# The decay's low-rank input on four column groups, summed by the next product

## The reference

```python
h = x * (1.0 + scale[:, None, :]) + shift[:, None, :]
(a_q, a_k, a_v, a_g, g_q, g_k, g_v, g_af, g_ab, ...) = jnp.split(h @ p['w_in'], pts, axis=-1)

def log_decay(pa, a2, ab):            # pa: tokens x 16, a2: 16 x 256
    z = (pa @ a2 + ab).astype(jnp.float32)
    return heads(jax.nn.log_sigmoid(z) / GLA_GATE_TEMP, GLA_DK)

... log_decay(paf, a2_f, ab_f), log_decay(pab, a2_b, ab_b)
```

## Time and profile before

| | |
|---|---|
| median of 3 runs | 1673.78 us (1673.46 to 1674.21) |
| the profiled execution's own time | 1673.7 us |
| its span | 1671.9 us |
| TensorE busy | 1612.8 us, 96% of the span |
| VectorE, ScalarE, GpSimd busy | 616.8, 423.3, 193.2 us |
| mean granted TensorE clock | 0.982 of full |
| bytes moved | 183.71 MB |

### The profile page before, as it was taken

The page is one execution under the profiler, slowest core; times in us unless marked ns, Lnnn a source line. Parts: engine busy times, 40 slices in busy tenths (PEclk is TensorE's granted clock), DMA queues, the critical chain, the costliest instruction groups (busy, mean ns, idle before and its releaser), DMA issues.

```text
span 1671.9 us, 17017 instructions
## 1 busy us (share of the span) xinstructions
PE 1612.8 (96%) x6880; PEld 1056.8 (63%) x6880; DVE 616.8 (37%) x1398; ACT 423.3 (25%) x808; POOL 193.2 (12%) x272
## 2 busy tenths in 40 slices
PE   5999999999999999999999999889999999999997
PEld 2544454455444444464776888478899847889883
DVE  1033342464200002522334311355577215567821
ACT  3114325432200000003243320034232213423320
POOL 0132100120010011121201102110100011010001
PEclk7999999999999999999999999989999999999999
DMA  9324332211112113321232343513322223432230
GB/s 389 149 101 157 123 123 94 84 52 40 60 76 76 75 51 142 130 101 54 101 116 86 115 170 119 195 51 137 116 101 76 104 102 135 151 107 95 76 126 38
DMA packets 16930, 183.71 MB, mean 110 GB/s; under 512 B 2258, under 2 KB 2514, under 8 KB 4564
## 3 DMA queue, kind: packets, MB, share of 16 engines
q1 hardware_dynamic: 16852, 182.62, 29.0%
HBM read 181.56 MB, written 1.05 MB: 109 GB/s over the span
## 4 chain that ended last, share of the span: by engine, by line
PE 93%; ACT 3%; DMA 2%; DVE 1%; POOL 0%; issue 0%; POOLq 0%; SPq 0%; ACTq 0%; DVEq 0%
PE ps L665 90%; PE ps L712 4%; DMA arena<-in_wf 2%; ACT arena L1136 1%; DVE arena L1515 0%; ACT L1469 0%; ACT L1467 0%; DVE arena L1512 0%; POOL arena L2054 0%; POOL arena L2058 0%; ACT arena L1467 0%; ACT arena L1368 0%; ACT L1370 0%; ACT L1368 0%; ACT arena L1352 0%
## 5 line engine op out<-in xcount | busy, mean ns | idle before, releaser
L665 PE MATMUL ps<-arena 128*128 128x256 f32 (+7 forms) x6396 | 1561.7, 426 | 26.9 <-DMA arena<-in_wf 17.2
L665 PEld LDWEIGHTS ps<-arena 128*128 128x128 f32 (+3 forms) x6396 | 1001.6, 186 | 551.7 <-issue 435.8
L2054 POOL TENSOR_TENSOR arena<-arena 128x256 f32<-128x256 f32 (+4 forms) x214 | 162.7, 779 | 1049.7 <-DVE arena L1515 648.8
L1515 DVE SCALAR_TENSOR_TENSOR arena<-arena 128x256 f32<-128x256 f32 (+3 forms) x443 | 211.1, 535 | 154.2 <-ACT arena L1241 41.1
L1136 ACT ACTIVATE arena<-ps 128x512 f32<-128x512 f32 (+2 forms) x274 | 142.6, 537 | 421.2 <-PE ps L665 398.2
L1515 DVE SCALAR_TENSOR_TENSOR arena<-arena,ps 128x256 f32<-128x256 f32 (+2 forms) x136 | 64.3, 482 | 389.6 <-PE ps L665 291.0
L1509 DVE TENSOR_TENSOR arena<-arena 128x512 f32<-128x512 f32 (+14 forms) x156 | 89.0, 592 | 120.5 <-ACT arena L1136 35.2
L712 PE MATMUL ps<-arena 128*128 128x128 f32 x480 | 75.7, 289 | 22.8 <-ACT arena L1136 18.2
L712 PEld LDWEIGHTS ps<-arena 128*128 128x128 f32 x480 | 58.4, 147 | 52.3 <-issue 27.1
L1307 ACT ACTIVATE arena<-ps 128x512 f32<-128x512 f32 (+1 forms) x24 | 13.5, 562 | 248.5 <-PE ps L665 248.5
L1512 DVE TENSOR_SCALAR arena<-arena 128x256 f32<-128x256 f32 (+9 forms) x181 | 64.9, 393 | 24.2 <-POOL arena L2054 17.0
(11 more groups left out here) (87 smaller groups left out, 306.0 us busy)
## 6 DMA issues: line engine op xcount, KB each, us to landing
arena<-in_wf SPq DMA_DIRECT2D x70, 2048.0 KB, 8.0
arena<-in_wf SPq DMA_DIRECT2D x20, 1024.0 KB, 6.7
arena<-in_wf SPq DMA_DIRECT2D x2, 1152.0 KB, 11.2
arena<-in_xinT SPq DMA_DIRECT2D x1, 2048.0 KB, 22.2
arena<-in_xin SPq DMA_DIRECT2D x4, 512.0 KB, 5.6
arena<-in_rp SPq DMA_DIRECT2D x2, 1024.0 KB, 10.3
arena<-in_consts SPq DMA_DIRECT2D x1, 1476.0 KB, 14.8
out<-arena SPq DMA_DIRECT2D x2, 512.0 KB, 2.6
```

The lines of the kernel that those rows point to most:

```text
L665: return e.matmul(o, l, r, start=start, stop=stop, skip_group_check=True)
L1515: return e.scalar_tensor_tensor(out=o, in0=x, scalar=s, in1=y, op0=op0, op1=op1)
L2054: return e.tensor_tensor(o, x, y, op)
```

## The change

The 8 products of `lr` are no longer added up in one place: product k goes to PSUM partitions 32 (k mod 4) to 32 (k mod 4) + 31, so each of the four column groups of the array has two of them, and the bank holds four partial sums below each other. ScalarE copies all 128 partitions to `TH2`. `z` multiplies all 128 partitions; its stationary tile holds the decay matrices four times below each other, so the product also adds the four parts. That tile stands in 512 new columns of the parameters, `PZ`, zero where nothing is named; `PM` keeps what the gating unit needs. The parameter transfer of each layer grows from 128x552 to 128x1064 values, and what stands behind `par` in SBUF moves by 512 columns.

```diff
-PA_BADA, PA_AB, PA_ON, PA_LG, PA_PM, PA_SW, PA_W = 0, 24, 28, 29, 40, 552, 1064
+PA_BADA, PA_AB, PA_ON, PA_LG, PA_PM, PA_PZ, PA_SW, PA_W = 0, 24, 28, 29, 40, 552, 1064, 1576
...
         PM = par[:, PA_PM:PA_PM + 512]
+        PZ = par[:, PA_PZ:PA_PZ + 512]
...
                         elif n == "lr":
-                            ins = feat(b, weights(f"a{l}kv", 8), 256, hT, 0, 512, [hk(l, k) for k in range(8)], 32)
+
+                            w = weights(f"a{l}kv", 8)
+                            for k in range(8):
+                                p.wait_ge(*hk(l, k))
+                                r = 32 * (k % 4)
+                                ins = mm(b[r:r + 32, :], w[:, k, 256:288], hT[:, k, :], k < 4, k >= 4)
...
-                        mm(bank("gla", l, "z", 2 * hp + d), PM[0:32, 256 * d + 128 * hp:256 * d + 128 * hp + 128],
-                           TH2[0:32, :], True, True).then_inc(gl_z.hit(l, 2 * hp + d), 1)
+                        mm(bank("gla", l, "z", 2 * hp + d), PZ[:, 256 * d + 128 * hp:256 * d + 128 * hp + 128],
+                           TH2, True, True).then_inc(gl_z.hit(l, 2 * hp + d), 1)
...
                         elif n == "lr":
-                            ins = copy(TH2[0:32, :], b[0:32, :])
+                            ins = copy(TH2, b)
...
-        pa[l][0:16, PA_PM:PA_PM + 256] = I["gla_a2_f"][l]
-        pa[l][16:32, PA_PM + 256:PA_PM + 512] = I["gla_a2_b"][l]
+        for r in range(0, 128, 32):
+            pa[l][r:r + 16, PA_PZ:PA_PZ + 256] = I["gla_a2_f"][l]
+            pa[l][r + 16:r + 32, PA_PZ + 256:PA_PZ + 512] = I["gla_a2_b"][l]

```

## The result

The changed kernel takes 1662.86 us (median of 4 runs, 1661.67 to 1663.28); the kernel before took 1673.62 us beside it (1672.62 to 1674.21). The ratio is 0.9935, 95% interval 0.9918 to 0.9952. It is faster by 10.8 us, 12.4 had been forecast; the time is inside the range and 1.6 us above the predicted one.

The account below looks back on a forecast made before the run. TensorE was taken to bound the kernel: 1673.7 - 10.3 (eight products) - 1.5 (z) + 0.4 (start) - 1.0 (clock) = 1661.3 us, range 1658.5 to 1666.6 us.

Parts of the forecast that it names:

- What bounds the kernel: Whole kernel: TensorE, busy 96% of 1671.9 us; what a stage costs TensorE is nearly everywhere what it costs the kernel.
- a wait takes the place: Rival, 8%: a VectorE or GpSimd chain paces one layer, its 5.1 us return as TensorE idle time; 1666.4 us.
- the slack in front of the k transposes: Layer 0, transposes waiting for VectorE's rotation: 8 us of 13 remain even if the rotation does not move.
- the 11 to 13 that were named as a sign: Sign in the profile after: TensorE's busy time down by 11 to 13 us, its waits as before.
- The eight products: Low-rank input of the decay, both layers: group from 6.99 to 1.85 us, saving 5.14 us a layer, 10.3 in both.
- The row of the 2-column products: Trace row of the modulation's eight-product group on four column groups: 1.83 us, used to price the new group.
- z: Product after the eight, on 128 partitions for 32: changes of tile shape vanish, 0.19 us a side, 1.5 us saved.
- ScalarE, new waits: Copy to TH2 on 128 partitions costs nothing more; no new wait is charged, at most one layer's 5.1 us.
- The start: Layer 0's larger parameter transfer delays the last modulation weights by 0.63 us at half clock; +0.4 us, bounds 0.3 and 0.65.
- The clock: Layer 1, half clock from 878.7 to 882.1 us behind narrow z: may go with full-width z; -1.0 us, bounds 0 and -1.7.
- the falls that I charged at zero: Half-clock falls elsewhere, 1.7 us each, either direction; as a rival, one or two, about 1658.5 or 1664.5 us, 7%.

Follow-up runs that it names:

- the packing alone: Against the kernel before: the eight 32-column products go to four column groups, z stays on 32 partitions with the old parameters; 1662.55 us, ratio 0.9936.
- the parameters alone: The kernel before with only the parameter transfers grown from 552 to 1064 columns, the added ones unused zeros; 1673.62 us, ratio 1.0002.
- the kernel before moved by 1.7 us: The kernel before with layer 1's first low-rank product issued twice more, four records, 1.72 us of TensorE; 1673.60 us, ratio 1.0001.
- the same move: The changed kernel with two more full-width products, 1.72 us of TensorE, ahead of layer 1's low-rank products; 1664.03 us, ratio 0.9943 to the kernel before.

## Why the prediction was right, and where it was off

- **What bounds the kernel.** Right. What left TensorE's stream left the kernel; its waits past the start are what they were, and no chain took the place of the products. The rival "a wait takes the place" did not happen: the slack in front of the k transposes went from 13.4 to 12.6 us only, since the rotation on VectorE moved by 4.3 us with the stream. Busy time fell by 13.9 us, outside the 11 to 13 that were named as a sign: the prediction had not allowed for a start with other stretches at half clock.
- **The eight products.** 1.85 us had been forecast and 1.85 and 1.86 us were measured; -10.26 us for -10.3. The row of the 2-column products was the right one to go by. The group's length also shows that the loads are hidden: 16 of them at 0.11 us in the open would make it 3.6 us. The Trainium skill, "TensorE: Matmul & The Clock Gate", Part 3 (Measured speedup vs the span model), has 2.38x for three column tiles; the prediction's estimate from it was a group of 2.2 us, and the trace does not agree, with 1.85 us. Nor does it agree with the rule of the Trainium skill, same page, Part 3 (What overlaps and what doesn't), that a load overlaps with running matmuls only when their row groups differ: here all use all rows, and the loads at 87.49 and 87.92 us go out while the group's matmuls run.
- **z.** -1.31 us, by the account of records, for -1.5. The change of shape costs 0.19 us at a side, as read; the third z of layer 1, for which I counted 0.19, won nothing that is left behind it. In the medians this gain cannot be seen: the packing alone is as fast.
- **ScalarE, new waits.** Nothing, as forecast.
- **The start.** The delay is 0.7 us with the parameters alone and 1.0 us in the profiled run of the changed kernel, for 0.63; +0.25 us are left of it for +0.4. That this is near is in part luck. Half of the 1.0 us is given back, as the prediction had it. Another 0.25 us went because the clock rose 0.5 us earlier than in the profile before; the prediction had kept that time as it was. The kernel with the parameters alone can't be told from the one before.
- **The clock.** The term that was wrong, in cause and in size. "With z on 128 partitions there are two full products in that place" was my reason for -1.0 us. The fall did go, -1.7 us, but full-width z were not needed for it: it is also gone with narrow z when the stretch lies elsewhere (the packing alone, the kernel before moved by 1.7 us), and it doesn't come back with two narrow z in the changed kernel. And the falls that I charged at zero, and gave a chance of 7% as a rival, took 1.85 us: +0.79 at the beginning of layer 1, +1.06 in the second block. Together the clock is worth -1.70 + 1.85 = +0.15 us in place of -1.0.

Summed: 0.25 - 10.26 - 1.31 + 0.15 = -11.2 us, the 11.1 us of the spans. The profiled run of the changed kernel took 1662.58 us, 1.3 us above the forecast: 1.15 us by the clock, 0.2 by z, -0.15 by the start. So the total came out as near as it did because the eight products, four fifths of the sum, were right; of the small terms the start was helped by the clock. That the extra half clock at the beginning of layer 1 comes from the shift is likely. In the seven profiles in which TensorE is 4.9 to 8.6 us ahead of the kernel before at 700 us it is 6.8 us long, in the other five, up to 4.3 us ahead, 3.4 us. No run singles it out. For the second block the cause stays open: there the same move changed no length, while kernels that stand within 0.5 us of each other at 1060 us (the kernel before and the one with the parameters alone, the packing alone and the whole change) have half-clock stretches of different lengths.

## What to carry to other kernels

Narrow products, here with 32 stationary columns in f32, cost as much as full ones when they run one behind the other: 0.44 us a record at either width. On four column groups eight of them took 1.85 us for 6.99. This needs a next product that can add the parts up; its own contraction over 128 partitions for 32 cost nothing here. Look for such sums in what already follows. And when a change is worth a per cent or less, part of what is measured is where half-clock stretches happen to fall: count those of both traces before a microsecond is given to a cause, and move the unchanged kernel by a microsecond or two as a control, over several executions.

## What the runs showed of the hardware

- Two orders in which the program goes through the column groups make no difference: 0,1,2,3,0,1,2,3 and 0,0,1,1,2,2,3,3 take 1.85 and 1.87 us.
- A product alone in another tile shape costs 0.39 us beyond its matmul time (0.78 us for two of them in layer 1), nearly half of its 0.86 us.
- 1.72 us of added work can cost nothing: the kernel before, with it and without, takes 1673.60 and 1673.43 us in one series. In the profiles the half clock behind the start costs 1.8 us less with it, summed over one stretch that went, one that came and three that changed.
- Executions of one kernel differ in the same way. Of 21 of the kernel before, the 7 with a mean granted clock of 0.984 or 0.985 took 1672.4 to 1673.1 us, the 11 with 0.982 took 1673.4 to 1674.3 us.
- 3.0 us won in a start at half clock (the fourth piece at 28.93 for 31.95 us) gave 3.2 us at the end by the medians and 2.4 us by the profiled spans; the clock also rose 2.2 us earlier. When the clock rises in the start differs from profile to profile, 43.2 to 47.7 us in twelve.
- Loads of column-tiled products go out one round ahead of their matmuls: eight at 87.04 us, four at 87.49, four at 87.92 us, with rounds every 0.43 us.
